# Two moved orders in a streaming hybrid encoder step: a bank operation of deferred gate pairs, and the load of the mixer's first weight tile

## What is computed

```python
def swiglu(x, wg, wu, wd):
    return (jax.nn.silu(x @ wg) * (x @ wu)) @ wd        # wg, wu: 1024 x 2816, wd: 2816 x 1024

x = x + 0.5 * swiglu(rms_norm(x, g_ffn1), w_ffn1_gate, w_ffn1_up, w_ffn1_down)
proj = einsum('bsd,de->bse', rms_norm(x, g_mix), w_in)  # w_in: 1024 x 4104
...
x = x + 0.5 * swiglu(rms_norm(x, g_ffn2), w_ffn2_gate, w_ffn2_up, w_ffn2_down)
```

## Time and profile before

| | us |
|---|---|
| median of 3 runs | 1048.23 |
| lowest, highest | 1047.16, 1049.45 |
| the profiled execution, its own time | 1048.64 |
| its span, first to last instruction | 1046.9 |
| PE busy in the span | 1034.8 (99%) |
| DVE busy | 791.3 (76%) |
| ACT busy | 514.7 (49%) |
| POOL busy | 215.8 (21%) |

### The profile page before, as it was taken

One profiled execution on the slowest core, in us unless ns is written; L12 is line 12 of the kernel. 1 busy time (PEld: TensorE's weight loads), 2 busy tenths in 40 slices (PEclk: granted clock), 3 DMA queues, 4 the chain that ended last, 5 costly groups with the idle time before them and its releaser, 6 DMA issues.

```text
span 1046.9 us, 20879 instructions
## 1 busy us (share of the span) xinstructions
PE 1034.8 (99%) x8235; PEld 1026.8 (98%) x8235; DVE 791.3 (76%) x1496; ACT 514.7 (49%) x943; POOL 215.8 (21%) x190
## 2 busy tenths in 40 slices
PE   9999999999999999999999999999999999999997
PEld 8999999999999999999999999999999999999996
DVE  6985589997899986655655556588568899789996
ACT  6453366644666664433222223445336664466654
POOL 1100221212122111310332223210012222222210
PEclk9999999999999999999999999999999999999998
DMA  8447787788878466445354223543777878887852
GB/s 228 118 80 177 169 178 168 170 182 170 183 161 176 98 139 136 76 68 82 68 81 75 68 74 69 142 91 86 177 162 162 187 160 171 179 178 167 175 108 97
DMA packets 217050, 142.13 MB, mean 136 GB/s; under 512 B 8684, under 2 KB 214676, under 8 KB 216824
## 3 DMA queue, kind: packets, MB, share of 16 engines
q1 hardware_dynamic: 160824, 110.98, 40.3%
q0 software_dynamic: 56048, 29.79, 22.3%
q10 hardware_dynamic: 80, 0.02, 0.0%
HBM read 135.80 MB, written 3.29 MB: 133 GB/s over the span
## 4 chain that ended last, share of the span: by engine, by line
PE 92%; DVE 3%; issue 2%; DMA 2%; ACT 1%; SPq 0%; DVEq 0%; ACTq 0%
PE dense L887 41%; PE dense L763 35%; PE core_banks L887 6%; PE core_banks L763 3%; PE dense L833 1%; DMA sum_ident<-sq 1%; PE core_banks L1130 1%; PE core_banks L1115 1%; PE core_banks L1133 1%; PE core_banks L1105 1%; DMA x_tok<-in_x_prompt 1%; DVE h_op L1823 1%; DVE w_lo L1781 1%; DVE h_raw L1811 0%; PE core_banks L1142 0%
## 5 line engine op out<-in xcount | busy, mean ns | idle before, releaser
L1318 ACT ACTIVATE w_hi<-w_src 128x512 fp32r<-128x512 f32 x182 | 113.2, 628 | 97.8 <-PE dense L887 55.8
L1318 ACT ACTIVATE w_hi<-w_raw 128x512 fp32r<-128x512 f32 x182 | 112.4, 629 | 77.7 <-PE dense L887 52.2
L887 PE MATMUL dense<-h_op,w_hi 128*128 128x272 f32 x768 | 147.9, 291 | 0.9 <-DVE h_op L1823 0.9
L1781 DVE TENSOR_TENSOR w_lo<-w_src,w_hi 128x512 fp32r<-128x512 f32 x182 | 124.6, 688 | 29.9 <-ACT w_hi L1318 28.1
L1781 DVE TENSOR_TENSOR w_lo<-w_raw,w_hi 128x512 fp32r<-128x512 f32 x182 | 123.9, 688 | 29.0 <-ACT w_hi L1318 27.0
L763 PE MATMUL dense<-xg_hi,w_hi 128*128 128x272 f32 x672 | 141.5, 292 | 0.0
L763 PE MATMUL dense<-xg_hi,w_lo 128*128 128x272 f32 x672 | 138.4, 288 | 0.0
L763 PE MATMUL dense<-xg_lo,w_hi 128*128 128x272 f32 x672 | 138.1, 287 | 0.0
L887 PE MATMUL dense<-x_late_hi,w_hi 128*128 128x272 f32 x432 | 125.7, 291 | 0.0
L887 PE MATMUL dense<-x_op_hi,w_lo 128*128 128x272 f32 x432 | 124.5, 288 | 0.0
L887 PE MATMUL dense<-x_late_hi,w_lo 128*128 128x272 f32 x432 | 124.4, 288 | 0.0
(11 more groups left out here) (365 smaller groups left out, 2390.3 us busy)
## 6 DMA issues: line engine op xcount, KB each, us to landing
w_raw<-in_w_ffn_up SPq DMA_DIRECT2D x43, 512.0 KB, 4.9
w_src<-in_w_ffn_gate SPq DMA_DIRECT2D x36, 512.0 KB, 5.2
w_raw<-in_w_in SPq DMA_DIRECT2D x31, 512.0 KB, 8.6
w_src<-in_w_ffn_gate POOLq DMA_DIRECT2D x36, 256.0 KB, 5.5
w_raw<-in_w_ffn_up POOLq DMA_DIRECT2D x36, 256.0 KB, 5.8
w_src<-in_w_ffn_down SPq DMA_DIRECT2D x16, 512.0 KB, 5.4
w_raw<-in_w_ffn_down SPq DMA_DIRECT2D x16, 512.0 KB, 5.4
w_raw<-in_w_ffn_down SPq DMA_DIRECT2D x16, 384.0 KB, 6.2
```

Of the source, the lines that this page charges most:

```text
L887: last = nc.tensor.matmul(out, w[:, k, :], x, start=o in OPENS and k == 0 and m == 0, stop=k == KH - 1 and m == 2, skip_group_check=o not ...
L1318: nc.scalar.activation(block_of(w_hi, n, o), source(e, o), ACT.Copy).then_inc(block_hi, 1)
L1781: nc.vector.tensor_tensor(block_of(w_lo, n, o), source(g % 2, o), block_of(w_hi, n, o).bitcast(F32), ALU.subtract)\
```

## The change

Two orders change; no instruction is added or taken away. DVE's `gate_second` of a deferred gate pair moves from step 4 to the end of step 3, so that it stands ahead of `next_lo` 3 instead of behind it. SP's `in_first` moves from ahead of the down tiles to behind the three loads of pair 2's blocks, which stand behind the down tile with `j` = 3.

```diff
                 for p in PAIRS[0]:
                     load_pair(p)
-                if n == 0:
-                    sp.dma_start(in_first[:, :, :], w_rows(w_in)[:, :, 0:P]).then_inc(in_loaded, 16)
                 for j in range(DT):
                     load_down(n, j, w_rows(w_down))
                     if j == RAW - 1:
                         load_pair(PAIRS[1][0])
+                        if n == 0:
+                            sp.dma_start(in_first[:, :, :], w_rows(w_in)[:, :, 0:P]).then_inc(in_loaded, 16)
...
                     if o == 4:
                         if e == 0:
-                            gate_second(n, p)
+                            if not deferred:
+                                gate_second(n, p)
...
                             h_to_lo(n, k, h_o)
+                        if e == 0 and o == 3:
+                            gate_second(n, p)
                     if not (ends and o == 6):
                         next_lo(n, g, o)
```

## The result

The changed kernel takes 1050.0 us (median of 17 runs, 1047.48 to 1052.44). The kernel before, on the same chip, takes 1047.82 (17 runs, 1047.16 to 1049.45). The ratio is 1.0018, 95% interval 1.0011 to 1.0025: 0.18% slower, where 1045.6 us and 0.25% faster were predicted. It lies above the range's upper end, and within the 0.2% that the prediction called the same. The profiled execution took 1050.41 us with a span of 1048.6.

What follows compares the result with a forecast made beforehand. The prediction took PE, busy 99% of the span, as the bound, stopped twelve times by a late `gate_second`. 1048.23 us less 2.65 for DVE's order and 0 for moving `in_first` gave 1045.6 us, range 1044.2 to 1047.6.

Steps and rivals of the forecast that it cites:

- First step: In deferred gate pairs, `gate_second` ahead of `next_lo` 3 ends PE's wait at block 6: 2.65 us, low end 2.1.
- stop at block 4: DVE's wait at `product_done`, brought forward by the new order: covered by 0.27 us, cost 0.
- PE's twelve stops: PE's weight loads wait for `gate_second` at block 6, once per deferred gate pair; removing these waits gains 2.65 us.
- the low part of block 3: DVE's `next_lo` 3 begins 0.35 us later, but PE needs it over 6 us later: cost 0.
- PE's gap ahead of `down`: PE's 1.52 us gap at 82.29 us, waiting for ACT's last silu of the pair; forecast to stay.
- Rival 1: DVE paces the four chunks' ends, so each last deferred pair gains nothing: 1.7 us less, 1046.5 us; chance 0.11.
- One mark: Sign of a right forecast: DVE's idle time in the up pairs gets some 0.2 us shorter.
- Second step: Moving `in_first` behind pair 2's block loads: taken as 0, bounds -1.5 and +4.4 us.
- 100.0: Latest time in us at which the load of down tile `j` = 4 may land without stopping PE.
- Rival 4: `in_first` keeps its 14.2 us and delays down tiles 4 to 7; PE stops 4.4 us: 1050.0 us, chance 0.07.
- Rival 2: PE's stop at block 6 stays, through another late release or DVE waiting for block 4: 1048.2 us, chance 0.06.
- Rival 3: Early `in_first` traffic causes PE's gap ahead of `down`, so 1.52 us go as well: 1044.1 us, chance 0.04.

Runs made afterwards that it cites:

- the slow columns: Changed kernel, but `in_first` loads columns 3072 to 3199 of `w_in` instead of 0 to 127: 1049.58 us, ratio 1.0012 to the kernel before.
- the quick columns: Changed kernel, but `in_first` loads columns 3712 to 3839 of `w_in` instead of 0 to 127: 1044.85 us, ratio 0.9974 to the kernel before.
- the other rows: Changed kernel, but `in_first` reads its 512 KB from `w_ffn2_up`, rows 11264 B apart, instead of `w_in`: 1044.96 us, ratio 0.9969 to the kernel before.

## Why the prediction was wrong

**First step, `gate_second` ahead of the low part: right.** All of its reading held: DVE didn't stop at block 4, PE's twelve stops went, the low part of block 3 was missed by nobody. The size was 2.65 us by the stretches. The order alone gave 3.2 (1048.14 less 1044.97), and the runs with the order and no stop lie 2.8 to 3.3 below their kernels before. The 0.5 us above 2.65 is within the interval of the ratio, and PE's gap ahead of `down`, shorter in these profiled executions too, may be part of it. PE's waits at the chunks' ends stayed as they were: twelve before, and twelve after, of which the list gives four to `issue` (before, then the changed kernel):

```profile
PEld dense L887 <- DVE xT L1910: 3.3, 12, 0.4
PEld dense L887 <- DVE xT L1910: 1.7, 8, 0.2
PEld dense L887 <- issue: 1.5, 4, 0.4
```

Rival 1 (part of the gain lost at the chunks' ends) is refuted: the stretch behind the last deferred gate pair of each of the four chunks takes 9.03 us in the changed kernel, 9.25 or 9.26 before. One mark was wrong: DVE's idle time in the up pairs should have shrunk by 0.2 us, and it stayed at 0.47. DVE waits there for ACT and ACT for PE, so the whole pair moved forward.

**Second step, `in_first`: the step that failed.** The reading had most of the mechanism in it: what stands behind the tile in SP's queue, who waits for tile 4, and when (100.0). The term that failed is the delay. I took 1.7 to 7.9 us, by 305 GB/s and 66 GB/s; measured, it was 11.8. Two arguments for the smaller number were wrong. First, the 66 GB/s of the earlier trace rows was no lower bound of the transfer's rate: the first two of the eight microseconds still moved other loads' bytes, at 112 GB/s. Cut into windows of 2 us, the trace of before shows what was left:

```profile
56.00:58.00 2.00, 2.00 (x18) 2.00 (x17) 2.00 (x3) 0.72 (x2) 0.00 (x0) 1.00 0.55 52
58.00:60.00 2.00, 2.00 (x18) 2.00 (x17) 2.00 (x3) 0.98 (x2) 0.00 (x0) 1.00 0.53 46
60.00:62.00 2.00, 2.00 (x18) 2.00 (x17) 1.90 (x4) 0.73 (x1) 0.00 (x0) 1.00 0.65 56
```

At 46 GB/s, 512 KB take 11.4 us (an estimate from this row), and that is beyond the 9.8 at which the prediction let a stop begin. In the changed kernel 4 us at 40 GB/s stand in a row. Second, against the 14.2 us of the earlier trace rows I argued that they "include the block loads ahead of it in its present place". They do, for the first 5.2 us; but the new place has loads ahead of it as well, for 5.7 us, and the transfer lands 13.8 to 16.0 us after its issue in every place that was tried. The trace of before had one more sign: with `in_first` in its old place, POOL's two adding transfers of pair 1 took 13.6 us (median), and without it, in the changed kernel, 5.1:

```profile
w_raw<-in_w_ffn_up POOLq DMA_DIRECT2D x2, 256.0 KB, 13.6
w_raw<-in_w_ffn_up POOLq DMA_DIRECT2D x2, 256.0 KB, 5.1
```

**The slack was smaller than 9.8 us, too.** Two things took from it. PE's gap at 82 us, which the prediction left in place, closed to 0.3 us, so PE came to tile 4 1.4 us earlier than in the kernel before: a gain upstream that the late load took back. And DVE works in order: the low part of the late tile stands ahead of the add of L2150, which empties the bank of an earlier tile (in the chain from 103.81 to PE's start at 104.59, 0.8 us), so PE got the bank only after both. With 100.0 - 1.4 - 0.8 = 97.8 in the place of 100.0, a load at 101.98 gives the 4.2 us of stop.

**A stop isn't only its own length.** In the changed kernel and in the move alone, the 144 matmuls behind the stop took 19.7 us in place of 18.05, at a granted clock of 0.71 and 0.67 in the first 4 us. In the profiled execution of the slow columns the stop was 2.62 us, the clock stayed at 1.00, and that execution took 1047.0 us, where the median is 1049.58. The prediction had no term for it. The wide scatter of the change (1047.5 to 1052.4, against 1044.4 to 1045.8 with the order alone) goes with the clock: of its 17 executions, those with a mean granted clock of 0.997 or 0.998 took 1047.5 to 1047.7 us, those at 0.996 took 1048.7 to 1050.4, and those at 0.994 or 0.995 took 1050.9 to 1052.4. With the order and no stop, every execution is at 0.997 or 0.998. That the clock fell behind this stop in the executions that weren't profiled too is likely from this, and not shown; single executions of the kernel before are low as well (0.994 at 1055.57 us).

**The rivals.** Rival 4 is what happened, and its time, 1050.0 us, is the measured one, but not by its own sum, so the agreement is luck. It had a delay of 14.2 and a stop of 4.4 with nothing behind it; it was a delay of 11.8, a slack cut to 7.6, and 1.7 us of slower clock, against a gap that closed. Its chance of 0.07 was too low: the only row of the transfer's own duration said 14.2, and nothing in the trace said that it would be shorter elsewhere. Rival 2 is refuted by the order alone. Rival 3 (the early traffic is the cause of PE's gap at 82) isn't borne out: weight loads wait there 1.1 us with the order alone and the tile at its old place, 1.0 with the tile last, 1.1 with half of it, 0.3 with the quick columns, and 0.6 with the other rows; the gap doesn't follow the tile's place, and what sets it stays open.

**What beats both kernels**: the DVE order with `in_first` left where it was, or asked for behind the eighth down tile, from ACT's queue, or in two halves: 1044.8 to 1045.0 us, 0.3% below the kernel before.

## What to carry to other kernels

A transfer's duration isn't its bytes over the bandwidth of the stretch that it is moved to: look in the trace for its own time from issue to landing, for its rate in windows short enough to hold no other load's bytes, and for the time of transfers of the same shape from the same tensor, and take the longest as the bound until a row excludes it. A transfer that was slow by its addresses held up the loads of other queues here too, so put such a one where nothing with a near due time is asked for behind it, or split it. And work out the slack at the new pace: what the change gains upstream, and what the late engine has in order behind the late step, both come off it.

## What the runs showed of the hardware

- Two loads of 512 KB from the same rows of one tensor, 16416 B apart, 512 B from each, differ by nearly a factor of two with the columns: 8.3 and 15.9 us from issue to landing, at the same place in the queue. In the mixer the same two take 5.5 to 5.6 and 13.1 to 13.4 us in two kernels, the slow one with another load ahead of it for some 5 us.
- A slow transfer holds the DMA engines for the other queues: 40 to 69 GB/s in all in such a stretch, with the engines half busy; POOL's adding transfers took 16.4 and 17.6 us in place of 7.2 and 8.5, and in the run with `in_first` on ACT's queue a load of SP's kept ACT waiting for 10.90 us.
- In two profiled executions, with stops of PE of 2.6 and 4.0 us, the granted clock was 0.67 and 0.71 in the window from 104 to 108 us, in which PE had begun again; in a third, with a stop of 2.62, it stayed at 1.00.
